# Front of a hybrid block kernel: input loads reordered, adaptive units alternated, h built by channel blocks, two key units multiplied during the build

## The reference, cut to what matters

```python
def ada_params(cond, w_ada, b_ada):
    return jnp.split(jax.nn.silu(cond) @ w_ada + b_ada, 6, axis=-1)
...
def gdn_prep(qkv, ab, conv_w, a_log, dt_bias):
    qkv = jax.nn.silu(centred_conv(qkv, conv_w))
    q, k, v = jnp.split(qkv, 3, axis=-1)
...
    g_f = -jnp.exp(a_log[0])[:, None] * jax.nn.softplus(a_f + dt_bias[0][:, None])
...
    u_l, v_l, qkv_l, z_l, ab_l, ga_l, gb_l = jnp.split(h_l @ w_in, IN_SPLITS, axis=-1)
```

## Time and profile before

| | us |
|---|---|
| median of 3 runs | 1061.7 (1061.43 to 1061.73) |
| span of the profiled execution | 1062.4 |
| difference of the two | 0.7 |
| PE busy in that span | 894.9 |
| DVE busy | 647.0 |
| ACT busy | 520.6 |

### The profile page before, as it was taken

One profiled execution on the slowest core, in us unless ns is written; L12 is line 12 of the kernel. 1 busy time (PEld: TensorE's weight loads), 2 busy tenths in 40 slices (PEclk: granted clock), 3 DMA queues, 4 the chain that ended last, 5 costly groups with the idle time before them and its releaser, 6 DMA issues. The chain is left out here.

```text
span 1062.4 us, 14126 instructions
## 1 busy us (share of the span) xinstructions
PE 894.9 (84%) x5494; PEld 760.4 (72%) x5494; DVE 647.0 (61%) x837; ACT 520.6 (49%) x832; POOL 177.6 (17%) x323
## 2 busy tenths in 40 slices
PE   2899888988789987899776898994999999999991
PEld 0578777888668876688676787873778777778771
DVE  1277466443754447545346444757798887888774
ACT  2366542324523246332463222544777777877761
POOL 3102050012500124001204001001121111111002
PEclk9899989999899998999988899996999999999996
DMA  8555447431483315843444552691799999999984
GB/s 292 192 162 166 126 93 214 125 94 48 109 250 106 90 45 134 219 138 90 144 124 137 170 174 67 218 338 40 264 356 358 392 363 374 387 378 381 362 303 139
DMA packets 218893, 216.79 MB, mean 204 GB/s; under 512 B 33168, under 2 KB 154681, under 8 KB 218185
## 3 DMA queue, kind: packets, MB, share of 16 engines
q1 hardware_dynamic: 216089, 205.90, 59.8%
q0 software_dynamic: 2736, 9.96, 2.5%
HBM read 194.83 MB, written 21.00 MB: 203 GB/s over the span
## 5 line engine op out<-in xcount | busy, mean ns | idle before, releaser
L1907 DVE TENSOR_TENSOR w_lo<-raw,w_hi 128x2048 fp32r<-128x2048 f32 x96 | 222.9, 2330 | 48.6 <-ACT w_hi L1378 48.1
L2124 PE MATMUL bank<-hT,half_hi 128*128 128x256 f32 (+1 forms) x1024 | 235.4, 326 | 16.6 <-ACT staged L1075 13.1
L1378 ACT CAST w_hi<-raw 128x2048 fp32r<-128x2048 f32 x96 | 183.2, 1911 | 74.7 <-DMA raw<-in_w_e_dram 68.0
L2124 PEld LDWEIGHTS bank<-hT,half_hi 128*128 128x128 f32 x1024 | 173.9, 199 | 33.3 <-ACT staged L1075 14.1
L1508 DVE TENSOR_TENSOR half_lo<-half_raw,half_hi 128x1024 fp32r<-128x1024 f32 x88 | 108.5, 1236 | 102.1 <-ACT half_hi L977 101.8
L2124 PE MATMUL bank<-lane 128*128 128x128 f32 (+1 forms) x1072 | 142.2, 293 | 25.3 <-DMA lane<-inverse 14.0
L2124 PE MATMUL bank<-hT,half_lo 128*128 128x256 f32 (+1 forms) x512 | 163.2, 319 | 0.0
L2124 PEld LDWEIGHTS bank<-lane 128*128 128x128 f32 (+1 forms) x1072 | 130.7, 200 | 37.1 <-issue 19.9
L2124 PE MATMUL bank<-w_hi,window 128*128 128x512 f32 x480 | 155.3, 395 | 0.0
L2124 PEld LDWEIGHTS bank<-hT,half_lo 128*128 128x128 f32 x512 | 101.5, 198 | 5.9
L2124 PEld LDWEIGHTS bank<-w_hi,window 128*128 128x128 f32 x480 | 90.1, 188 | 19.2
(11 more groups left out here) (302 smaller groups left out, 1294.5 us busy)
## 6 DMA issues: line engine op xcount, KB each, us to landing
raw<-in_w_e_dram SPq DMA_DIRECT2D x96, 1024.0 KB, 7.9
half_raw<-in_w_in_dram SPq DMA_DIRECT2D x64, 512.0 KB, 4.2
half_raw<-in_w_ada_dram SPq DMA_DIRECT2D x32, 512.0 KB, 4.2
raw<-in_w_ada_dram SPq DMA_DIRECT2D x8, 1024.0 KB, 10.1
expert_rows<-y_out POOLq DMA_DIRECT2D x15, 512.0 KB, 7.7
dense<-staged SPq DMA_DIRECT2D x32, 128.0 KB, 3.0
lane<-inverse SPq DMA_DIRECT2D x16, 256.0 KB, 5.4
lane<-inverse_turned SPq DMA_DIRECT2D x16, 256.0 KB, 4.7
```

The costliest lines, as they stand in the source:

```text
L1378: act.copy(e_hi[n % WBUF][:, :], raw[n % RING][:, :]).then_inc(s["hi_ready"], 1)
L1907: dve.tensor_tensor(e_lo[n % WBUF][:, :], raw[n % RING][:, :], e_hi[n % WBUF][:, :].bitcast(F32), ALU.subtract)\
L2124: return nc.tensor.matmul(dst, lhsT, rhs, start=start, stop=stop)
```

## The change

Seven things, all before or just after the point where h is complete:

1. SP loads ctx and x first, then the small rows, then the adaptive units. The gate weights (`ab_raw`), gate rows and `ada_bias` move behind all adaptive units, and the first two half units move between adaptive units 3 and 4.
2. Adaptive units alternate shift and scale of 256 channels; the 16 sums become four groups of 4, and DVE's three gain instructions run four times on a quarter.
3. Affine and split of h run by pairs of blocks, between the adaptive units.
4. `first_channels` multiplies the first two key units block by block of h, both banks at once, in place of `channels(0, ...)` and `channels(1, ...)`. The number and shape of the 48 products are the same.
5. The gate products come after these, and their columns, `gate_acts`, `gate_decays`, `gate_totals`, `gate_exps` and `gate_weights` follow among the convolutions of the first units.
6. `taps(1)` and `center(1)` move ahead of `silu(0)` and of the next split.
7. A few semaphores are shared, which changes no order.

```diff
@@ -519,25 +531,19 @@
...
-            def half(n):
-                r = n % HRING
-                if n >= HRING:
-                    if n - HRING in ada_entries:
-                        sp.wait_ge(s["ada_taken"], ada_entries.index(n - HRING) + 1)
-                    else:
-                        sp.wait_ge(s["half_split"], SPLITS.index(n - HRING) + 1)
-                view = eight(half_raw[r]) if half_shape[n] == 8 else two(half_raw[r])
-                load(view, HALVES[n], half_landed[r])
+                b, kind = n // 2, n % 2
+                load(wide(raw[n % RING]), ada_v[:, :, D * kind + 256 * b:D * kind + 256 * b + 256], landed[n % RING])
+                if n == 3:
+                    load(conv_rows[:, :], b_conv_w[0].rearrange("j (k p) -> (j k) p", p=P), s["landed_conv"])
+                    half(0)
+                    half(1)
+            half(2)
+            load(ab_raw[:, :, :], in_v[:, :, COL_AB:COL_AB + 32], s["landed_ab"])
+            half(3)
+            for n2, v in enumerate((b_A_log, b_dt_bias)):
+                load(gate_row[:, n2, :, :].rearrange("p d h -> p (d h)"),
+                     v[0].rearrange("d h -> (d h)").partition_broadcast(P), s["landed_gate"])
+            load(ada_bias[:, :], b_ada[0, 2 * D:6 * D].rearrange("(m n) -> m n", n=N), s["landed_gate"])
...
+            affine(0)
+            affine(1)
+            ada_rows(1)
             high(0)
             high(1)
-
...
+            affine(2)
+            affine(3)
+            copy_conv()
+            ada_rows(2)
+            affine(4)
+            affine(5)
+            ada_rows(3)
+            affine(6)
+            affine(7)
...
@@ -1512,33 +1525,65 @@
                 if m + 2 < len(SPLITS):
                     low(m + 2)
 
+            ada_ps = bank[7][:, 256:288].rearrange("p (m s) -> p m s", s=2)
+
+            def gains(b):
+                ks = slice(2 * b, 2 * b + 2)
...
+            def split_h(kc):
+                dve.wait_ge(s["h_affine"], kc + 1)
+                own.after(dve.tensor_copy(hT_hi[:, kc, :], h_full[kc]))
+                dve.tensor_tensor(hT_lo[:, kc, :], h_full[kc], hT_hi[:, kc, :].bitcast(F32), ALU.subtract)\
...
+            gains(0)
+            split_h(0)
+            split_h(1)
+            gains(1)
             low(0)
             low(1)
-            dve.wait_ge(s["ab_sum"], 1)
...
+            split_h(2)
+            split_h(3)
+            gains(2)
+            split_h(4)
+            split_h(5)
+            gains(3)
+            split_h(6)
+            split_h(7)
...
@@ -1746,18 +1791,20 @@
             i = j = 0
             ahead(CHAN_AT[j, 0])
             taps(0)
-            gate_sums()
+            gate_inputs()
             ahead(CHAN_AT[j, 1])
+            taps(1)
             silu(0)
-            taps(1)
-            gate_weights()
+            gate_decays()
             ahead(CHAN_AT[j, 2])
             silu(1)
             taps(2)
+            gate_sums()
             ahead(CHAN_AT[j, 3])
             normed(0, 0)
             silu(2)
             taps(3)
+            gate_weights()
...
@@ -2132,46 +2179,91 @@
             pe.wait_ge(s["cols_copied"], 2)
 
             def turn_x(kc):
-                if kc >= 6:
-                    pe.wait_ge(s["h_affine"], kc - 5)
+                if kc == 0:
+                    pe.wait_ge(s["x_normed"], TILES)
+                if kc >= 2:
+                    pe.wait_ge(s["h_affine"], kc - 1)
                 for t in range(TILES):
-                    ins = turn(bank[XT_BANK[kc]][:, t * P:(t + 1) * P], x_nat[:, t, kc * P:(kc + 1) * P])
+                    ins = turn(bank[XT_BANK[kc % 2]][:, t * P:(t + 1) * P], x_nat[:, t, kc * P:(kc + 1) * P])
                 ins.then_inc(s["xT_ready"], 1)
...
+            def ada_sums(b):
+                pe.wait_ge(s["ada_row_copied"], b + 1)
+                if b:
+                    pe.wait_ge(s["gains_ready"], b)
+                for kind in range(2):
+                    for k in range(2):
+                        m = 8 * kind + 2 * b + k
+                        at_ = N * b + 256 * kind + P * k
+                        ins = mm(bank[7][:, 256 + 2 * m:258 + 2 * m], ada_row[:, at_:at_ + P], fold[:, 0:2])
+                ins.then_inc(s["ada_summed"], 1)
+
+            def first_channels(kc):
+                if kc == 0:
+                    pe.wait_ge(s["half_split"], 2)
+                pe.wait_ge(s["h_split"], kc + 1)
+                for n in range(2):
+                    dst, hi, lo = bank[n][:, :], eight(half_hi[n]), eight(half_lo[n])
+                    mm(dst, hi[:, kc, :], hT_hi[:, kc, :], kc == 0, False)
+                    mm(dst, hi[:, kc, :], hT_lo[:, kc, :], False, False)
+                    ins = mm(dst, lo[:, kc, :], hT_hi[:, kc, :], False, kc == KC - 1)
+                    if kc == KC - 1:
+                        ins.then_inc(s["half_used"], 1)
+
+            def gate_products():
+                pe.wait_ge(s["landed_ab"], 16)
+                for kc in range(KC):
+                    j = kc % 4
+                    ins = mm(bank[4][32 * j:32 * j + 32, :], ab_raw[:, kc, :], h_full[kc], kc < 4, kc >= 4)
+                ins.then_inc(s["ab_part_sum"], 1)
+
+            def gate_columns():
+                pe.wait_ge(s["ab_copied"], 1)
+                for t in range(TILES):
+                    ins = mm(bank[7][:, 32 * t:32 * t + 32], ab_part[:, t * P:(t + 1) * P], fold[:, :])
+                ins.then_inc(s["ab_sum"], 1)
+
+            ada_unit(0)
+            ada_unit(1)
+            ada_unit(2)
+            ada_sums(0)
+            turn_x(0)
+            turn_x(1)
+            ada_unit(3)
+            ada_sums(1)
+            turn_x(2)
+            turn_x(3)
+            pe.wait_ge(s["landed_conv"], 16)
+            turn(bank[4][:, 0:120], conv_rows[:, :], 120).then_inc(s["cols_ready"], 1)
+            ada_unit(4)
+            first_channels(0)
+            first_channels(1)
+            ada_unit(5)
+            first_channels(2)
+            first_channels(3)
+            ada_sums(2)
+            turn_x(4)
+            turn_x(5)
+            ada_unit(6)
+            ada_unit(7)
+            turn_x(6)
+            turn_x(7)
+            ada_sums(3)
+            for kc in range(4, KC):
+                first_channels(kc)
+            gate_products()
 
             def gate_totals():
                 pe.wait_ge(s["gate_dve"], 2)
@@ -2182,7 +2274,6 @@
```

203 lines of the change are left out of this document (90 added, 113 removed).

## The result

| | before | changed |
|---|---|---|
| median of the runs compared | 1061.7 (1061.4 to 1066.8, 4 runs) | 1050.3 (1045.6 to 1053.0, 4 runs) |
| ratio, 95% interval | | 0.9864 [0.9816, 0.9913] |
| span of the profiled execution | 1062.4 | 1043.7 |

The change makes the kernel faster by 1.4% [0.9 to 1.8]. The two medians of the table alone would give 0.9892; the later comparisons of the same two kernels give 0.9863 and 0.9865 (experiments 1 and 10). An execution that took over 1.5% more than the fastest of its kernel is left out of the ratios. The profiled execution of the changed kernel took 1045.6, 1.9 more than its span and 4.7 less than the median.

What follows compares the result with a forecast made beforehand. Up to 57 us PE mostly waits in one chain of loads, sums, gains and affine. Third unit 15.1 us earlier, 2.1 returned on DVE: 1062.4 - 13.0 = 1049.4 profiled, 0.7 less for the median, 1048.7 (range 1044.5 to 1056).

Steps and rivals of the forecast that it cites:

- Loads: SP's queue: ctx and x at 0.93, narrow loads behind unit 7; units 0 to 7 land from 11.0 to 33.2.
- 3 us or more before PE comes: Adaptive units 4 to 7: each lands at least 3 us before PE needs it, so none is waited for.
- x ready: Squares, power and scaling of x, after the rows (8.3) and their silu (0.3): ready at 18.4.
- PE's list, T0: End of the first two key units on PE, summed from instruction prices: 51.2, between 48.0 and 52.6.
- Gate products: On PE after the first key units: 2.1 us taken, 4.9 upper; third unit starts at T0 + 4.0, 55.2.
- The lag: DVE's gate work between convolutions delays the first query transpose, PE waiting before the second `turn_back`: 2.1 of 15.1 us returned.
- The sum: Whole kernel: 1062.4 - 13.0 = 1049.4 for the profiled execution, 0.7 above the median, so 1048.7.
- low in blocks 4 to 7: Rival: PE's clock low from 38 us on; T0 55.7 to 58.6, gain 8.5 to 5.6, 1053 to 1056; chance 0.22.
- The gate work did hurt: Rival: gate work hurts more, gate products at upper bound and DVE's idle kept; gain 8.1, 1053.6; chance 0.08.
- Slower: Rival: low clock carried into the third and fourth unit, once T0 passes 64.2; 1072; chance 0.03.

Runs made afterwards that it cites:

- experiment 1: The changed kernel again, no edit: 1047.3 us, ratio 0.9863.
- experiment 10: The changed kernel a third time, no edit: 1051.2 us, ratio 0.9865.
- experiment 8: Changed kernel with gate decays behind the first pair's last silu, totals behind the second z product, then sums, exponentials and weights: 1057.5 us, ratio 0.9898.
- experiment 11: Changed kernel with fitted unused identity products in PE's waits, late decays, totals ahead of the second z product, sums and weights behind the z gates: 1046.6 us, ratio 0.9845.
- experiment 6: Changed kernel with DVE's gate inputs and decays and ACT's copy and gate activations ahead of the first convolution again: 1064.2 us, one run.
- experiment 4: Changed kernel with all eight blocks of the first two key units behind the last adaptive sums: 1052.1 us, one run.
- experiment 7: Changed kernel with unused identity products in PE's waits: 36 ahead of the rows, 4 ahead of unit 0, 8 ahead of units 1 and 2: 1044.3 us, ratio 0.9801.
- experiment 12: Changed kernel with ctx, x and narrow loads behind adaptive unit 0 and all first key blocks behind the last sums: 1061.9 us, ratio 0.9962.
- experiment 2: The kernel before again, no edit: 1064.6 us, one run.
- experiment 9: Changed kernel with unused identity products in counts fitted to PE's waits (26, 2, 6, 6, and 3 before x transposes and second sums): 1047.4 us, ratio 0.9844.
- experiment 5: Changed kernel with ctx, x and all narrow loads behind adaptive unit 0 as before, half units still behind unit 3: 1051.3 us, ratio 0.987.

## Why the prediction was right

The forecast of 1048.7 (range 1044.5 to 1056) met 1050.3; a gain of 13.0 was said, the medians differ by 11.4, and the ratios of the three comparisons, 0.9864, 0.9863 and 0.9865, are 14.4 us of 1064. The mechanism held: an earlier front moves everything behind it, less a lag on DVE. Its sizes were off, and partly against each other.

- **Loads.** Units 0 to 2 start at 11.4, 14.0 and 16.7; 11.0, 13.7 and 16.5 were said. Units 3 and 4 landed at 19.4 and 25.3 (19.2 and 25.0 said), by issue and time to landing. The cover of "3 us or more before PE comes" was 1.3 for unit 4, because PE came at 26.6 and not at 28.0. No load was waited for after 20 us, as said, and none before by more than 1.1.
- **x ready.** 19.5 instead of 18.4 (15.84 + 3.69): the rows' silu ended at 9.8, not 8.6.
- **PE's list, T0.** This term failed in size: 51.2 was chosen between 48.0 (fast prices throughout) and 52.6; measured are 46.6, 46.9 and 47.5. The 52.6 took slow adaptive units to 30 us and slow transposes (1.93) to the end, as in the timeline of before; the fast prices began at 24. Besides, four sums take 1.05 and later 0.95, where 1.4 was read from the row of sixteen, which lay partly at half clock; 46.6 lies below even the bound that had been called warm throughout. The first key product (30 said, 28.45), unit 7 (42 to 44 said, within the two units that end at 39.0) and the third unit (55 said, 50.12) are early by the same cause.
- **Gate products.** Two units' worth, 2.1 said, 1.92 measured; from T0 to the third unit 3.5 instead of 4.0.
- **The lag.** Said 2.1 of 15.1 returned, measured 1.7 of 20.1. The query transpose was put at T0 + 30.7 "at least" (T0 + 31.2 in the point) and came at T0 + 30.4 each time. But it does not lie where the prediction put it. PE does not wait at the second `turn_back`: of its 1.2 us up to there 1.06 is more busy time (19.58 against 18.52), of which the gate totals are 0.6 (59.11 to 59.70). They now stand behind the third unit (at 64.00, ahead of the second, before) and were not in the sum. Waits of PE are 0.15 up to there and 0.27 up to the query transpose. DVE's decays started at 55.75 without waiting for the tables, as said. In experiments 8 and 11, with the gate work gone from both engines, 1.0 us of the 1.7 comes back; they do not part PE's share from DVE's.
- **The sum.** "That execution lies 0.7 above the median" compared a span with a time. The time is 1.9 above the span in every run where both are known, so this execution took about 1064.3, 2.6 above the median then known. The two slips cancel: 1064.3 - 13.0 is 1051.3 for a profile, and less 2.6 it is 1048.7 for a median, the same forecast. But a median of three runs says little here: the four later groups of 11 to 13 runs of before had medians from 1063.6 to 1066.6.
- **The rivals.** The clock was not low in blocks 4 to 7 of any run; slow prices lasted or came back before them, up to 36 us at the latest (experiments 4, 7, 8, 10, 11 and 12), mostly where the prediction had counted them anyway. In the changed kernel the fast prices began at 22 to 24, in a mix of sums, transposes and an adaptive unit, with no dense product near. In experiment 10 the clock fell under just such a mix, from 18 us on, after units with waits of 0.7 to 1.0 between them. The Trainium skill, "TensorE: Matmul & The Clock Gate", Part 4, says that full clock does not engage for transposes. These two traces do not decide on it, since thin products stood among the transposes. The kernel before does speak against it, and in both of its profiles: under transposes alone the grant rose from 0.50 to 1.00, by 48 us and, in experiment 2, by 46. The gate work did hurt where it is not moved (experiment 6, 11 us); moved, it did not. "Slower" was never near: it needed T0 past 64.2.

So the direction and the mechanism were right, and that the point came within 2 us of the median is luck. The front gained 18.5 where 13.0 was said (15.5 to 18.5 over the profiles of both kernels); the span of the profiled execution was 1043.7 where 1049.4 was said; and the median of the four runs lay 4.7 us above its own profiled execution.

## What to carry to other kernels

When a front becomes a chain of short steps, read the price of each kind of instruction at both clocks, and ask of each execution which one it had: here that alone moves the same instructions by 3 us. Before you credit an edit with a gain, split the stretch into busy and idle time: the early key blocks took no idle time off PE. Judge an edit of 10 us in a kernel of 1060 by a landmark just behind it, and only then by the time: the stretch behind varied by 12 us between executions of the same code. And when loads are moved ahead, read each landing from its issue and its time to landing, in the kernel itself: a wait of 1.7 us for the fifth unit in the filled kernel does not put the changed one at its edge, since there the unit lands 1.4 us sooner.

## What was not expected of the hardware

The granted clock in the windows of the changed kernel is 1.00 from 0 to 34 us, yet adaptive units take 1.93 us to 18.6 and 1.07 from 26.6 on. In the profiles of this kernel the column told nothing until the clock had changed once; the durations of a repeated instruction did. With products in its waits PE was at 1.07 by 12.1 us (experiment 9); without, they began between 16 us (experiment 10, where they ended again) and 31 us (experiment 8).

Products that fill waits were not free for the loads: units 3 and 4 landed 1.4 us later in all three filled kernels (experiments 7, 9 and 11).

The narrow loads behind x took 1.9 us more in one profile of before than in another, and 1.3 more in experiment 5 than in 12, with the same issues.
